# Windowed-attention scores: one f32 pass with zero-padded queries, or two fp32r passes over stacked halves

## What is computed

```python
q = rms_norm(a_q.reshape(b, s, A_KV_HEADS, grp, HEAD_DIM), q_norm)
k = rms_norm(a_k.reshape(b, s, A_KV_HEADS, HEAD_DIM), k_norm)
s = jnp.einsum('nbqkgd,nbskd->nbkgqs', qb, kw) * (d ** -0.5)
s = s - slopes * dist            # masked outside the window
m = jnp.maximum(jnp.max(s, -1), sink)
p = jnp.exp(s - m)               # den = sum(p) + exp(sink - m)
o = jnp.einsum('nbkgqs,nbskv->nbqkgv', p, vw) / den
```

## Time and profile before

| | |
|---|---|
| median of 3 runs | 2744.35 us (2741.24 to 2745.07) |
| profiled execution | 2741.32 us, its span 2739.5 us |
| mean granted TensorE clock | 0.996 |
| PE matmul busy | 2644.2 us (97% of the span) |
| DVE busy | 1565.9 us (57%) |
| ACT busy | 1232.0 us (45%) |

### The profile page before, as it was taken

The page is one execution under the profiler, slowest core; times in us unless marked ns, Lnnn a source line. Parts: engine busy times, 40 slices in busy tenths (PEclk is TensorE's granted clock), DMA queues, the critical chain, the costliest instruction groups (busy, mean ns, idle before and its releaser), DMA issues. The chain is left out here.

```text
span 2739.5 us, 35859 instructions
## 1 busy us (share of the span) xinstructions
PE 2644.2 (97%) x12974; PEld 2215.0 (81%) x12974; DVE 1565.9 (57%) x3276; ACT 1232.0 (45%) x2510; POOL 1.5 (0%) x6
## 2 busy tenths in 40 slices
PE   5999999999999989999999999999999999899999
PEld 4899987777877778888879998877788777788887
DVE  5564577544566556464764546775455566464645
ACT  5455555444544334242454555544445443342423
POOL 0000000000000000000000000000000000000000
PEclk9999999999999999999999999999999999999999
DMA  5212223222121323333342122221222213232333
GB/s 167 77 55 78 81 63 92 62 65 82 55 72 52 101 86 92 100 93 100 93 123 70 47 86 74 80 83 54 70 78 68 63 47 108 85 100 93 99 93 100
DMA packets 143872, 225.26 MB, mean 82 GB/s; under 512 B 15046, under 2 KB 69458, under 8 KB 142802
## 3 DMA queue, kind: packets, MB, share of 16 engines
q1 hardware_dynamic: 135842, 201.85, 24.7%
q10 hardware_dynamic: 7856, 21.12, 2.1%
HBM read 210.29 MB, written 12.65 MB: 81 GB/s over the span
## 5 line engine op out<-in xcount | busy, mean ns | idle before, releaser
L1413 DVE TENSOR_TENSOR s_wl<-s_raw,s_wh 128x1024 fp32r<-128x1024 f32 (+2 forms) x376 | 453.7, 1207 | 382.0 <-ACT s_wh L937 380.6
L937 ACT ACTIVATE s_wh<-s_raw 128x1024 fp32r<-128x1024 f32 (+2 forms) x376 | 392.3, 1043 | 440.8 <-PE bank L565 423.3
L565 PE MATMUL bank<-s_hTh,s_wh 128*128 128x512 f32 x1216 | 520.4, 428 | 3.6 <-DVE s_hTl L1517 3.6
L565 PE MATMUL bank<-s_hTh,s_wl 128*128 128x512 f32 x1216 | 474.7, 390 | 0.0
L565 PE MATMUL bank<-s_hTl,s_wh 128*128 128x512 f32 x1216 | 473.9, 390 | 0.0
L565 PE MATMUL bank<-s_wh,s_hTh 128*128 128x512 f32 (+1 forms) x1088 | 469.6, 432 | 3.5 <-DVE s_early L1530 3.3
L565 PE MATMUL bank<-s_wh,s_hTl 128*128 128x512 f32 (+1 forms) x1088 | 426.0, 392 | 0.0
L565 PE MATMUL bank<-s_wl,s_hTh 128*128 128x512 f32 (+1 forms) x1088 | 425.4, 391 | 0.0
L565 PEld LDWEIGHTS bank<-s_hTh,s_wh 128*128 128x128 f32 x1216 | 228.6, 188 | 70.9 <-issue 27.3
L1241 ACT ACTIVATE s_work<-s_work,s_stat 128x128 f32<-128x128 f32 (+3 forms) x320 | 167.5, 524 | 257.7 <-DVE s_work L1929 113.5
L565 PEld LDWEIGHTS bank<-s_hTl,s_wh 128*128 128x128 f32 x1216 | 228.8, 188 | 66.6 <-issue 24.4
(11 more groups left out here) (189 smaller groups left out, 3376.9 us busy)
## 6 DMA issues: line engine op xcount, KB each, us to landing
s_raw<-in_w_in SPq DMA_DIRECT2D x168, 512.0 KB, 3.6
s_raw<-in_ffn_w_up SPq DMA_DIRECT2D x176, 256.0 KB, 3.1
s_raw<-in_ffn_w_down SPq DMA_DIRECT2D x44, 512.0 KB, 3.7
s_raw<-in_w_branch SPq DMA_DIRECT2D x32, 512.0 KB, 3.7
s_raw<-in_w_o SPq DMA_DIRECT2D x16, 512.0 KB, 3.7
x_keep<-s_work ACTq DMA_DIRECT2D x2, 2048.0 KB, 6.9
s_raw<-in_w_in SPq DMA_DIRECT2D x16, 256.0 KB, 2.9
gate_keep<-s_early ACTq DMA_DIRECT2D x4, 1024.0 KB, 4.3
```

The costliest lines, as they stand in the source:

```text
L565: last = mm(PJ[b][:, 0:width], st, mv, start=i == 0 and n == 1, stop=i == ntiles - 1 and n == 3 * chunks)
L937: a(wh[:, k % 3, 0:n], raw[:, s, 0:n], ACT.Copy).then_inc(*hi_split.up(own))
L1413: v.tensor_tensor(wl[:, k % 3, 0:n], raw[:, k % 2, 0:n], wh[:, k % 3, 0:n].bitcast(F32), ALU.subtract).then_inc(*tile_split.up(own))
```

## The change

The scores of pattern A use split operands in fp32r. Rows 64:128 of the keys now hold the keys' low half. The stationary operand of the first pass holds the queries' high half in all 128 rows, so this pass gives hi·hi + hi·lo. That of the second pass holds the queries' low half in rows 0:64 and zeros in rows 64:128, so it gives lo·hi. ACT writes the high half twice per head pair (`mine` and `other`), DVE subtracts for the low half, and at the start of A in each layer ACT copies zeros. The tile `q_two` lies where D's keys lay.

```diff
+    with nc.sbuf_tensor("s_stacked", [P, AD + 15872], F32R) as stacked:
+        pass
-    kA, vA = in_work(AD + 14336, 1024, g=2), in_work(AD + 15360, 512, t=4)
+    kA, vA = stacked[:, AD + 14336:AD + 15360].rearrange("p (g n) -> p g n", g=2), in_work(AD + 15360, 512, t=4)
+    q_two = stacked[:, AD + 4096:AD + 6144].rearrange("p (c h s n) -> p c h s n", c=4, h=2, s=2)
...
 # PE
+                        if name == "A":
+                            pe.wait_ge(*q_stacked.at(l, pads_of(name, step)))
...
+                def stacked_scores(u, out):
+                    lo, hi, _mid = near_keys(u)
+                    h = u % 8
+                    return [(out[:, P * lo:P * hi], q_two[:, h // 2, h % 2, s, :],
+                             kA[:, h // 4, P * lo:P * hi], s == 0, s == 1) for s in range(2)]
...
-                yield from attention("A", near_scores(lambda h: kA[:, h // 4, :]),
+                yield from attention("A", stacked_scores,
...
-                                     heads_in(57, 72), keys=near_keys, tile_of=out_tiles)
+                                     heads_in(57, 72) + [q_zeroed.at(l, 2)], keys=near_keys, tile_of=out_tiles)
...
 # ACT
+                def stacks_of_a():
+                    first, slot = done, slots("A")
+                    for piece in range(8):
+                        t, g = piece // 2, piece % 2
+                        yield slot[4 * piece - 4][1] + 0.8 * slot[0][2] if piece >= 2 else slot[0][1] - 0.5
+                        if piece == 0:
+                            act.wait_ge(*td_dve.at(l, 57))
+                        act.wait_ge(*s_ready.at(l, first + 4 * piece - 4 if piece >= 2 else first))
+                        if piece == 0:
+                            for half in range(2):
+                                act.wait_ge(*own.done(l))
+                                a(q_two[64:128, :, half, 1, :], q_pad[64:128, :, 0, :], ACT.Copy).then_inc(*q_zeroed.up(own))
+                        for half in range(2):
+                            mine, other = slice(64 * half, 64 * half + 64), slice(64 - 64 * half, 128 - 64 * half)
+                            for part in (mine, other):
+                                act.wait_ge(*own.done(l))
+                                a(q_two[part, 2 * g:2 * g + 2, half, 0, :], qA[mine, 2 * g:2 * g + 2, P * t:P * t + P],
+                                  ACT.Copy).then_inc(*(act_step if part is mine else q_hi).up(own))
...
-                yield from tiles_of("A", qA, 57, by_pair)
+                yield from stacks_of_a()
+                done += WINDOW["A"][2]
...
 # DVE, in the transposes after kv, ahead of line 1795
+                    key = kA[64:128, :, P * t:P * t + P]
+                    dve.wait_ge(*own.done(l))
+                    v.scalar_tensor_tensor(key, src[64:128, 0:256].rearrange("p (c n) -> p c n", c=2), prm[64:128, ROW["ak"]:ROW["ak"] + 1],
+                                           key.bitcast(F32), ALU.mult, ALU.subtract).then_inc(*dve_step.up(own))
...
+            def stacks():
...
+                slot, n = slots("A"), 0
+                for piece in range(8):
+                    t, g = piece // 2, piece % 2
+                    yield (slot[4 * piece - 4][1] + 0.8 * slot[0][2] if piece >= 2 else slot[0][1] - 0.5) + 0.1
+                    for half in range(2):
+                        n += 1
+                        mine = slice(64 * half, 64 * half + 64)
+                        dve.wait_ge(*q_hi.at(l, n))
+                        dve.wait_ge(*own.done(l))
+                        v.tensor_tensor(q_two[0:64, 2 * g:2 * g + 2, half, 1, :], qA[mine, 2 * g:2 * g + 2, P * t:P * t + P],
+                                        q_two[mine, 2 * g:2 * g + 2, half, 0, :].bitcast(F32), ALU.subtract).then_inc(*q_stacked.up(own))
```

More of the change, by code:

```diff
@@ L162 @@
 B_NORM = WINDOW["B"][1]
-PADS = dict(C0=16, C1=8, C2=8, A=16, B=16)
+PADS = dict(C0=16, C1=8, C2=8, B=16)
 def pads_of(name, u):
-    return u + 1 if PADS[name] == 8 else 4 * (u // 8) + 2 * (u % 8 // 4) + 2
+    return u + 1 if PADS.get(name) == 8 else 4 * (u // 8) + 2 * (u % 8 // 4) + 2
 def build(nc, io):
@@ L794, in attention @@
                             pe.wait_ge(*q_padded.at(l, pads + pads_of(name, step)))
+                        if name == "A":
+                            pe.wait_ge(*q_stacked.at(l, pads_of(name, step)))
                         pe.wait_ge(*s_biased.at(l, first + step))
-                        for out, st, mv in scores_of(step, S1):
-                            last = mm(out, st, mv, start=True, stop=True)
+                        for out, st, mv, start, stop in scores_of(step, S1):
+                            last = mm(out, st, mv, start=start, stop=stop)
                         last.then_inc(*s_ready.up())
@@ L839, in attention_b @@
                         pe.wait_ge(*s_biased.at(l, first + step))
-                        for out, st, mv in scores_of(step, S1):
-                            mm(out, st, mv, start=True, stop=True).then_inc(*s_ready.up())
+                        for out, st, mv, start, stop in scores_of(step, S1):
+                            mm(out, st, mv, start=start, stop=stop).then_inc(*s_ready.up())
             def token_values(v_of, width, places, keys=all_keys):
@@ L858, in scores_of @@
                         h = u % 8
-                        return [(out[:, P * lo:P * hi], q_pad[:, h // 2, h % 2, :], k_of(h)[:, P * lo:P * hi])]
+                        return [(out[:, P * lo:P * hi], q_pad[:, h // 2, h % 2, :], k_of(h)[:, P * lo:P * hi], True, True)]
                     return scores_of
+                def stacked_scores(u, out):
[3 more added lines that the diff above has]
+                             kA[:, h // 4, P * lo:P * hi], s == 0, s == 1) for s in range(2)]
                 def residue_scores(j):
                     return lambda h, out: [(out[:, P * r:P * r + P], q_pad[:, r, h % 2, :],
-                                            CK[j][:, h // 2, P * r:P * r + P]) for r in range(RES)]
+                                            CK[j][:, h // 2, P * r:P * r + P], True, True) for r in range(RES)]
                 def residue_values(j):
@@ L871, in b_scores @@
                     n = 4 * (u % 2) + (u % 8) // 2
-                    return [(out[:], q_pad[:, n // 2, n % 2, :], kT[:, n // 2, :])]
+                    return [(out[:], q_pad[:, n // 2, n % 2, :], kT[:, n // 2, :], True, True)]
                 def heads_in(turns_done, evacuated):
@@ L1960, in attentions @@
                 yield from attention_b()
-            return norm1(), dense(), turns(), attentions(), c_combine()
+            return norm1(), dense(), turns(), stacks(), attentions(), c_combine()
         together(setup_rest(), splits(), *[shifted(stream, TOTAL * l) for l in range(DEPTH) for stream in layer(l)])
```

9 lines of the change are left out of this document (6 added, 3 removed).

## The result

The changed kernel takes 2755.93 us (median of 5 runs, 2755.0 to 2757.21), the kernel before 2744.35 on the same chip (5 runs, 2741.24 to 2746.06): ratio 1.0044, interval 1.0033 to 1.0055. The prediction was 2737.8, faster. It missed in the direction, and the time lies above its range.

What follows compares the result with a forecast made beforehand. PE was taken to bound the kernel, busy 97% of the span. A gain of 8.5 us less 5.25 of waits per layer, 6.5 net for two layers, taken from the median 2744.35 gave 2737.8; range 2731 to 2746.

Steps and rivals of the forecast that it cites:

- The gain: PE's scores in A: two fp32r passes take 0.37 instead of 0.70 us and 0.26 instead of 0.46, saving 8.5 per layer.
- the rival at 2759: Scores in A: exposed weight loads make passes no cheaper, kernel 15 us slower; chance 0.06.
- The start of A: PE waits 2.0 us for DVE's subtraction at the first score, 0.66 at the second: 2.7 us lost per layer.
- Piece 2: Two more ACT copies and DVE's subtraction delay the bias PE waits for: 1.4 us lost per layer (0.9 to 1.8).
- Piece 5: ACT's copies delay the copy out of TA, bias and division, then the next tile's values: 0.6 us (0 to 1.2).
- Pieces 3, 4, 6 and 7: ACT's or DVE's idle time ahead of the next need exceeds a microsecond: 0.15 us lost in all per layer.
- kv: Transposes after kv: DVE's new operation stands before one PE waits for, 0.4 us more per layer (0 to 0.8).
- The sum: Per layer 5.25 us lost against 8.5 won: 3.25 net, 6.5 us won for two layers.
- The clock: The start's stall may drop PE's clock once per layer, 0 to 3.4 us; left out of the likeliest case.
- No change: Rival: stalls plus clock falls, or ACT's delay meeting PE at more pieces (4 us per layer, 2746); chance 0.29.

Runs made afterwards that it cites:

- pool_all: `pool_early` with GpSimd also doing the queries' subtractions and zero copies, so ACT and DVE have in A what they had before the change: 2734.53 us, ratio 0.9963.
- early: Changed kernel with the zero copies and piece 0's copies due earlier, piece 1's due later, DVE's subtractions moved with them: 2748.55 us, ratio 1.0017.
- f32_pass: Changed kernel with all new ACT and DVE work kept, but each score one f32 matmul, queries' low half left out: 2758.87 us, ratio 1.0051.
- again: The changed kernel run once more, unaltered: 2754.37 us, ratio 1.0046 to the kernel before.
- no_subs: Changed kernel without DVE's subtractions of the queries and PE's waits for them, queries' low half zero: 2749.0 us, ratio 1.0023.
- no_key: Changed kernel without DVE's operation on the keys' low half in the transposes after kv: 2750.41 us, ratio 1.0025.
- pool_early: Changed kernel with the edits of `pool` and `early` together: 2734.99 us, ratio 0.9968.
- pool: Changed kernel with the second copy of the queries' high half moved from ACT to GpSimd, which reads the first copy: 2741.12 us, ratio 0.9992.
- base: The kernel before, unchanged, run again to see its scatter: 2742.16 us, ratio 0.9995.
- all_f32: `pool_all` with each score one f32 matmul, queries' low half left out: 2747.64 us, ratio 1.0019.
- all_no_key: `pool_all` without DVE's operation on the keys' low half: 2730.95 us, ratio 0.9956.

## Why the prediction was wrong

**The gain: right, a little high.** 8.5 us per layer was forecast, 8.0 measured. The 384-column score was put at 0.37 us and takes 0.43. The 256-column score was put at 0.26 us. The timelines show 0.32 behind transposes, and 0.23 between dense matmuls in `pool_all`, from 653.87 to 654.33 less 0.23:

```profile
653.87 0.40 PE L819 MATMUL bank<-s_stacked 128*128 128x256 f32 x2
654.10 0.40 PE L584 MATMUL bank<-s_gTh,s_wh 128*128 128x512 f32 x1
654.33 0.40 PE L584 MATMUL bank<-s_gTl,s_wh 128*128 128x512 f32 x1
```

Two passes in 0.23 us are 0.12 each, while a dense load is recorded with 189 ns. Loads were not exposed, and the rival at 2759 fell, though the time came near its number. The Trainium skill ("TensorE: Matmul & The Clock Gate", section "The mechanism" in the part on packing small matmuls) has two sentences on this. Its list of what overlaps says that loads overlap matmuls in flight only where the row group differs; these passes use all rows in both operands and overlap all the same, so the trace disagrees. The sentence ahead of the list also has loads into a background weight buffer pulled ahead, and by that one the overlap was to be expected; that it is this buffer no run here shows.

**The start of A: right.** Forecast 2.0 and 0.66 us lost, 2.7 in all. Measured 1.79 and 0.42 of idle time, with 0.24 for each wait 2.7 in all. `early` takes 2.2 off A in layer 0 (142.01 against 144.25), as a shorter wait for the bias stays. It was called the step most likely to fail.

**Piece 2: right in size.** Forecast 1.4 lost; the bias wait grew from 0.73 to 0.86, and a wait for the copy out of TA, 1.06, came ahead of it: 1.2 more idle time, and 0.24 for the wait that is new make 1.4.

**Piece 5: too low.** Forecast 0.6; the wait for the output bank grew from 1.11 to 1.85, and a short one of 0.19 us for the copy out of TA, ahead of it, is new and costs 0.24 besides: 1.2 in all, the upper bound.

**Pieces 3, 4, 6 and 7: the step that failed.** "ACT's or DVE's idle time ahead of the next need is over a microsecond; I set 0.15 in all." The trace shows 0.68 at 696.94, 0.57 at 743.66 and 1.84 at 766.08, 3.1 together and 3.8 with 0.24 for each. The first and the last are waits for the output bank, which the prediction priced at piece 5 alone. Two things were left out. The idle microsecond was measured against the old PE: the new one has saved most of 8 us by slot 27, and the work of ACT and DVE that it needs there hasn't moved forward as much. And idle time on an engine counts only where it isn't itself waiting for another link of the same chain.

The chain behind the wait at 766.08 (ACT and DVE, layer 0) starts with the four copies of piece 7, where before there were two:

```profile
755.34 1.75 ACT L1302 ACTIVATE s_stacked<-s_work 64x256 fp32r<-64x256 f32 x4
...
758.58 0.38 ACT L1243 ACTIVATE s_work<-bank 128x256 f32<-128x256 f32 x1
...
759.90 0.48 DVE L1970 CUSTOM_DVE_ANT_0 s_work<-bank,s_near,s_sink 128x256 f32<-128x256 f32 x1
...
761.11 0.58 ACT L977 ACTIVATE s_work<-bank 128x512 f32<-128x512 f32 x1
...
763.02 0.29 ACT L1243 ACTIVATE s_work<-bank 128x128 f32<-128x128 f32 x1
...
763.61 0.48 DVE L1970 CUSTOM_DVE_ANT_0 s_work<-bank,s_near,s_sink 128x256 f32<-128x256 f32 x1
...
765.25 0.69 DVE L2003 TENSOR_TENSOR s_work<-bank,s_stat 128x512 f32<-128x512 f32 x1
```

The copies push ACT's copy out of TA, that pushes DVE's, the bias behind it and the exponential; then ACT squares and copies a dense block's bank twice (L977 and L979, four in a row from 761.11) ahead of the next copy out of TA, and the same order on DVE puts bias, a reduction for the dense block and the division behind it. ACT is idle for 1.45 us ahead of 760.41 and for 0.83 ahead of 764.14, but both times it waits for DVE's bias, which waited for ACT: such idle time absorbs nothing. In `pool_all` the same chain runs in 8.1 us from the end of the copies to the division (747.29 to 755.34; here 757.09 to 765.25, 8.2), with two copies of ACT at its head, and PE waits 0.27 us; in `f32_pass`, with four copies, it waits 0.71.

**kv: too low.** Forecast 0.4, measured 1.1 per layer, and 1.8 in `again`: the new operation (0.49 us) delays the low half for which PE waits (1.01 instead of 0.5), and the next operation too.

**The sum.** Forecast losses 5.25 per layer; measured 2.7 + 1.4 + 1.2 + 3.8 + 1.1 = 10.2. Against 8.0 of gain this makes 2.2 lost per layer, 4.4 in two, where 6.5 won was forecast. The lengths say nearly the same: without the clock A grew by 1.0 us in layer 0 (144.25 - 1.7 - 141.52) and 0.2 in layer 1 (145.07 - 3.4 - 141.51), where some of the slow clock overlaps the waits, and kv by 2.2, in all 3.4. The behaviour behind it is that the terms don't add up: gain and waits were summed as if independent, and the gain itself is what meets ACT's and DVE's late work. The pair of experiments shows it, 3 us against 13 for the same edit.

**The clock: left out, and it was not small.** The prediction bounded it by 0 to 3.4 us and gave it to a rival. The mean clock costs 8 us; in the profiled execution 5.1 of it lies in A, in three stretches of 3.4 us at the lower level, one in layer 0 and two in layer 1:

```profile
2040.00:2044.00 4.00, 3.69 (x11) 3.05 (x12) 0.87 (x5) 1.99 (x8) 0.00 (x0) 0.57 0.46 131
2094.00:2099.00 5.00, 5.00 (x19) 4.09 (x19) 4.04 (x18) 1.49 (x4) 0.00 (x0) 0.66 0.41 108
```

3.4 and 8 make 11.4, and 11.6 is the measured loss. The profile of `again` has three such stretches in A as well, those of `no_subs` and `no_key` too, `early` and `pool_early` have two, `pool` and `f32_pass` one, and before, `base`, `pool_all`, `all_f32` and `all_no_key` none. So the falls in A come with its long waits. The other 3 us lie outside A, and no run here settles what causes them: `base` has a fall there that the change didn't make. The means of whole kernels say the same less sharply: 0.9919 to 0.9930 for those with 7 to 10 waits of PE in A of layer 0, 0.9931 to 0.9944 for those with 4 to 6, 0.9942 and 0.9948 for the two with 2.

**"No change", the rival nearest to what happened,** named the right mechanism (ACT's delay meets PE at more pieces, with one or two clock falls) and gave it 0.29. Its price, 4 us per layer, was right for the three late waits (3.8). But piece 5, kv and the clock came on top, and no case joined them.

## What to carry to other kernels

When the engine that sets the end is made faster, read the slack of its helpers against the new engine and not the old: walk from each added operation to the next need with the saved time taken off, because a gain that meets a late operand turns into waiting there and doesn't offset anything. Look up in the program what a waiting instruction needs: the releaser that a profile names can be one that only ended at the same moment. Do one run with the delay and without the gain, and one with the gain and without the delay, before judging either: the edit was worth 3 us in one setting and 13 in the other. If an engine stands idle, as GpSimd did here with 1.5 us of work in 2750, prepare operands there before giving them to one that feeds the critical path, and forecast a stall near 2 us with its possible fall of the clock in the likeliest case.

## What the runs showed of the hardware

Left alone, GpSimd is no slower than ACT at a copy of 64x256 that moves the data between the halves of the partitions: in `pool_all` 394 ns at the median, where ACT's take 412 to 419. With DVE at work beside it it is: the mean there is 484 ns, and in `pool`, where DVE subtracts at the same time, the median is 480. Its subtraction takes 735 ns, DVE's 420. From the view by line of `pool_all` (minimum, median, maximum in ns, first and last start):

```profile
L542 POOL CAST s_stacked<-s_stacked x32: 392/394/1279, 647.5 to 2099.3; 64x256 fp32r<-64x256 f32 x32
...
L544 POOL TENSOR_TENSOR s_stacked<-s_work,s_stacked x32: 724/735/1588, 648.0 to 2099.6; 64x256 fp32r<-64x256 f32 x32
```

The maxima are collisions with DVE. In the timeline a weight split of DVE, 1.22 us elsewhere, and a subtraction of GpSimd lie over each other, and both are long:

```profile
647.55 1.42 DVE L1458 TENSOR_TENSOR s_wl<-s_raw,s_wh 128x1024 fp32r<-128x1024 f32 x1
...
647.98 1.58 POOL L544 TENSOR_TENSOR s_stacked<-s_work,s_stacked 64x256 fp32r<-64x256 f32 x1
```

The Trainium skill ("SBUF — State Buffer", section "Who interferes with whom") states that a DVE operation with both inputs in SBUF and a GpSimd operation that reads SBUF exclude each other for a whole instruction; the trace agrees. It costs little here, since GpSimd has time: the 17 splits in A of layer 0 take 1236 ns in the mean, against 1220 in the changed kernel.
